# A three-block layer stack: the first two slabs multiplied without their shift, scale and norm sums in 32-column tiles, the last norm by tokens, the top-k mask on VectorE

## The reference

```python
cond = silu(c)
for i in (0, 1):                                        # first block
    sh1, sc1, g1, sh2, sc2, g2 = split(cond @ ada_w[i] + ada_b[i], 6)
    h = rms_norm(x, norm_mix[i]) * (1 + sc1) + sh1
    x = x + g1 * (stick_breaking(h, w_in, w_out) if i == 0 else dsa(h, ...))
    h = rms_norm(x, norm_ffn[i]) * (1 + sc2) + sh2
    x = x + g2 * conv_ffn(h, w_up, conv_w, conv_b, w_down)
# second block: the same frame with window attention + HGRN, and conv_ffn on the gate half
return rms_norm(x, final_norm_g)

# in dsa: 64 keys are kept for each query; of 16 heads
logits = where(selected, q @ k.T * scale + rel_bias, -1e30)
```

## Time and profile before

| | |
|---|---|
| median of the runs | 1215.47 us |
| profiled execution | 1215.8 us, of which 1214.1 us is the span from first to last instruction |
| PE | 1163.4 us busy (96%) |
| DVE | 543.6 us busy (45%) |
| ACT | 250.1 us busy (21%) |
| mean granted TensorE clock | 0.982 |
| DMA | 234.04 MB, 193 GB/s on average |

### The profile page before, as it was taken

The page is one execution under the profiler, slowest core; times in us unless marked ns, Lnnn a source line. Parts: engine busy times, 40 slices in busy tenths (PEclk is TensorE's granted clock), DMA queues, the critical chain, the costliest instruction groups (busy, mean ns, idle before and its releaser), DMA issues.

```text
span 1214.1 us, 13985 instructions
## 1 busy us (share of the span) xinstructions
PE 1163.4 (96%) x5765; PEld 1001.1 (82%) x5765; DVE 543.6 (45%) x1056; ACT 250.1 (21%) x458; POOL 23.5 (2%) x82
## 2 busy tenths in 40 slices
PE   3899999999999999998999999999999999999997
PEld 2688888888888878877888888888788888888885
DVE  6255554555564546332455546464733231111113
ACT  2122323000000244542300000025423320000002
POOL 1000140000000000000000000000000000000000
PEclk8899999999999999989999999999999999999998
DMA  9977827787868452270678787754341345353510
GB/s 347 297 260 252 300 74 275 260 312 254 308 236 302 138 70 91 83 243 1 237 254 313 251 310 262 268 184 139 110 133 36 104 131 182 110 202 105 195 47 35
DMA packets 154161, 234.04 MB, mean 193 GB/s; under 512 B 8761, under 2 KB 126577, under 8 KB 154097
## 3 DMA queue, kind: packets, MB, share of 16 engines
q1 hardware_dynamic: 154097, 233.13, 57.0%
HBM read 231.67 MB, written 1.44 MB: 192 GB/s over the span
## 4 chain that ended last, share of the span: by engine, by line
PE 94%; DVE 3%; SPq 1%; ACT 1%; issue 1%; DMA 1%; ACTq 0%; DVEq 0%
PE PS L591 49%; PE PS L658 18%; PE PS L612 7%; PE PS L602 5%; PE PS L752 2%; PE PS L577 2%; PE PS L993 1%; PE PS L563 1%; DVE ada_acc L1476 1%; DMA ffn_work<-in_final_norm_g 1%; PE PS L1067 1%; PE PS L785 1%; PE PS L922 1%; PE PS L768 1%; PE PS L804 0%
## 5 line engine op out<-in xcount | busy, mean ns | idle before, releaser
L591 PE MATMUL PS<-hT,slot 128*128 128x256 f32 x2736 | 606.2, 380 | 4.4 <-ACT hT L1176 3.1
L591 PEld LDWEIGHTS PS<-hT,slot 128*128 128x128 f32 x2736 | 520.1, 191 | 77.4 <-issue 6.8
L658 PE MATMUL PS<-act,slot 128*128 128x256 f32 x1056 | 239.2, 380 | 1.5 <-DVE act L1591 1.5
L658 PEld LDWEIGHTS PS<-act,slot 128*128 128x128 f32 x1056 | 200.1, 190 | 30.9 <-DVE act L1591 2.3
L1562 DVE TENSOR_SCALAR ffn_work<-PS,pcol 128x256 f32<-128x256 f32 x100 | 50.7, 540 | 314.3 <-PE PS L591 314.2
L1476 DVE SCALAR_TENSOR_TENSOR ada_acc<-ada_slot,cond,ada_acc 128x1024 f32<-128x1024 f32 x126 | 161.5, 1282 | 6.2 <-DMA ada_slot<-in_ada_w 0.6
L1228 ACT ACTIVATE ffn_work<-ffn_work 128x256 f32<-128x256 f32 x66 | 27.6, 418 | 615.1 <-DVE ffn_work L1572 615.1
L612 PE MATMUL PS<-oT,slot 128*128 128x256 f32 x384 | 89.5, 395 | 6.2 <-DVE oT L1788 6.2
L612 PEld LDWEIGHTS PS<-oT,slot 128*128 128x128 f32 x384 | 75.6, 199 | 18.4 <-DVE oT L1788 6.9
L602 PE MATMUL PS<-xg,slot 128*128 128x257 f32 (+1 forms) x256 | 57.4, 381 | 2.4 <-DVE xT L1526 2.4
L602 PEld LDWEIGHTS PS<-xg,slot 128*128 128x128 f32 (+1 forms) x256 | 47.6, 187 | 11.3 <-issue 4.0
(11 more groups left out here) (250 smaller groups left out, 744.3 us busy)
## 6 DMA issues: line engine op xcount, KB each, us to landing
ada_slot<-in_ada_w SPq DMA_DIRECT2D x144, 512.0 KB, 7.9
slot<-in_ffn_w_up SPq DMA_DIRECT2D x44, 1024.0 KB, 11.5
slot<-in_ffn_w_down SPq DMA_DIRECT2D x22, 1024.0 KB, 4.9
slot<-in_w_up SPq DMA_DIRECT2D x22, 1024.0 KB, 5.1
slot<-in_sb_w_in SPq DMA_DIRECT2D x12, 1024.0 KB, 7.3
slot<-in_w_in SPq DMA_DIRECT2D x11, 1024.0 KB, 5.1
slot<-in_w_down SPq DMA_DIRECT2D x11, 1024.0 KB, 4.9
slot<-in_dsa_w_in SPq DMA_DIRECT2D x10, 1024.0 KB, 5.3
```

The costliest lines, as they stand in the source:

```text
L591: last = mm(PS[:, bank, half * T:half * T + T], slot[s][:, k, m * P:(m + 1) * P], x[:, k, :], start=k == 0, stop=k == KC - 1)
L658: last = mm(PS[:, c // 2, (c % 2) * T:(c % 2) * T + T], w[:, j_odd * D + c * P:j_odd * D + (c + 1) * P], act[:, j_odd, :], start=start and ...
```

## The change

1. **Start.** Scale sums: the eight pieces of vector 1 go straight to PE, as 32-column matmuls with cond broadcast as weights (L815 of the new file), and DVE no longer passes over them. The first two slabs are multiplied by the scaled, unshifted x (`project_unshifted`), while DVE adds up vector 0 (shift). Then `shift_products` multiplies the shift by the two slabs in 32-column tiles (L616), ACT copies the rows out of PSUM, and one more matmul for each bank adds them to every token (L624). The parameter rows are issued from ACT's queue instead of SP's, slabs 0 and 1 are loaded before vector 0, and the three slabs of pass 1 have slots 3 to 5.
2. **Norm sums.** `norm` puts the eight partial sums into four positions of 32 columns; ACT copies them to SBUF, and one matmul with `quarter` (`norm_total`) adds the four. It stands behind the second matmul of the raw product that follows. GpSimd builds `quarter` before it signals `consts_ready`.
3. **dsa mask.** `sel_b` and L926 are gone; DVE adds the fp32 mask to the position bias of each pair, two additions for each pair (`masked`), and `logits` reads the masked bias.
4. **Older chunks.** In the last two pairs `was_read(1, 1)` waits for the last `mix` but one; PE starts 5 chunks of n=0, then chunk 5 of n=0 and 6 chunks of n=1, then the sixth chunk of both and 7 of n=2.
5. **Last norm.** PE transposes xT itself, chunk by chunk as it is updated; ACT sums the squares of 512 features at a time from PSUM, DVE multiplies by the inverse root and the gain (a row broadcast to all partitions, loaded during the last FFN) from PSUM, and SP stores four pieces of 256 KB.

Behind the last `mix`, 18 matmuls on older chunks now stand before the first that needs its result; before, all that followed needed it. The diff, cut to its core:

```diff
+        def sb_slot(i, s):
+
+            return s + (3 if i == 1 else 0)
...
-            load_rows(FIRST_ROWS, params_loaded)
+            load_qkv(0, (0, 1))
             load_ada(0, 0)
-            load_qkv(0)
+            load_qkv(0, (2,))
+            load_qkv(1, (0, 1))
...
+            load_ada(0, 2, range(0, 5))
+            load_qkv(1, (2,))
+            load_ada(0, 2, range(5, KC))
+            load_qkv(2, (0, 1))
+            load_ada(0, 3, range(0, 5))
+            load_qkv(2, (2,))
+            load_ada(0, 3, range(5, KC))
+            load_qkv(3, (0,))
+            load_out(0, range(2))
+            load_ada(0, 4, range(0, 5))
+            load_qkv(3, (1,))
+            load_out(0, (2,))
+            load_ada(0, 4, range(5, KC))
+            load_qkv(3, (2,))
+            load_ada(0, 5)
...
+            load_ffn_step(2, 0, 0)
+            sp.wait_ge(mixed_ready, 1)
+            g = A["final_norm_g_2"]
+            sp.dma_start(final_g[:, :], bass.AP(tensor=g.tensor, offset=g.offset, ap=[[0, P], [1, D]])).then_inc(final_loaded, 16)
+            load_ffn(2, 1)
...
+            step(pool.memset(quarter[:, :], 0.0))
+            for n in range(4):
+                step(pool.affine_select(out=quarter[:, :], in_=quarter[:, :], compare_op=ALU.not_equal, fill=1.0,
+                                        base=-32 * n, pattern=[[0, P]], channel_multiplier=1))
...
+            def shift_mods():
+
+                bk("mods_full").next()
+                pe.wait_ge(ada_used[KC - 1], bk(f"ada_used{KC - 1}").next())
+                acc = ada_acc[:, 0:D].rearrange("p (c j) -> p c j", c=KC)
+                for n in range(4):
+                    last = mm(PS[32 * n:32 * n + 32, 7, T:2 * T], ones[:, 0:32], acc[:, :, 32 * n:32 * n + 32],
+                              start=True, stop=True, skip_group_check=True)
+                last.then_inc(mods_full, 1)
...
+            def shift_products():
+
+                pe.wait_ge(shift_ready, 1)
+                for s in range(2):
+                    for k in range(KC):
+                        q = k % 4
+                        last = mm(PS[32 * q:32 * q + 32, 4 + s, 0:SLAB], mod[:, k:k + 1].to_broadcast([P, 32]), slot[s][:, k, :],
+                                  start=k < 4, stop=k >= 4, skip_group_check=True)
+                        if s == 1 and k == 0:
+                            last.then_inc(slot_used[0], 1)
+                    last.then_inc(rows_full, 1)
+                for s in range(2):
+                    pe.wait_ge(rows_ready, s + 1)
+                    for m in range(2):
+                        last = mm(PS[:, 2 * s + m, 0:T], shift_rows[:, s, m * P:(m + 1) * P],
+                                  lane[:, 0:1].to_broadcast([P, T]), start=False, stop=True)
+                        if s == 0 and m == 0:
+                            last.then_inc(slot_used[1], 1)
+                    last.then_inc(unit_full[s], 1)
...
-                    last = mm(PS[:, bank, 0:T], ones[:, :], hT[:, c, :], start=c == 0, stop=c == KC - 1)
+                    q = c % 4
+                    last = mm(PS[32 * q:32 * q + 32, bank, 0:T], ones[:, 0:32], hT[:, c, :], start=c < 4, stop=c >= 4,
+                              skip_group_check=True)
                     if c == 0 and free_slot is not None:
                         last.then_inc(slot_used[free_slot], 1)
-                last.then_inc(stat_full, 1)
+                last.then_inc(part_full, 1)
+
+            def norm_total(bank=4):
+
+                pe.wait_ge(part_ready, bk("part_ready").next())
+                mm(PS[:, bank, 0:T], quarter[:, :], part_sum[:, :], start=True, stop=True).then_inc(stat_full, 1)
...
+            def project_unshifted(bank, s, m, by_chunk=False):
+
+                for k in range(KC):
+                    if by_chunk:
+                        pe.wait_ge(scaled_ready, k + 1)
+                    mm(PS[:, bank, 0:T], slot[s][:, k, m * P:(m + 1) * P], oT[:, k, :], start=k == 0, stop=False)
...
+                    if k == 2 and total is not None:
+                        norm_total(total)
...
-            norm(FIRST)
-            mods(0, 3)
-
-            def sb_query(by_chunk=False):
-                arrived(0)
+            for k in range(KC):
+                pe.wait_ge(ada_loaded[k], 16)
+                acc = ada_slot[k].rearrange("p (c j) -> p c j", c=KC)
+                for n in range(4):
+                    last = mm(PS[32 * n:32 * n + 32, 6, T:2 * T], cond[:, k:k + 1].to_broadcast([P, 32]),
+                              acc[:, :, 32 * n:32 * n + 32], start=k == 0, stop=k == KC - 1, skip_group_check=True)
+                last.then_inc(ada_used[k], 1)
+                if k == 4:
+                    norm(FIRST)
+                elif k == 6:
+                    norm_total()
+            bk(f"ada_used{KC - 1}").next()
...
+            for s in range(2):
+                arrived(s)
+                fill(s)
+                project_unshifted(2 * s, s, 0, by_chunk=s == 0)
+                project_unshifted(2 * s + 1, s, 1)
+            shift_mods()
+            shift_products()
+            sb_value(0)
...
-                    mm(PS[:, 4 + e, 0:P], qh[:, b, e, 0:P], kn[:, 0:P], start=False, stop=False, skip_group_check=True)
-                    mm(PS[:, 4 + e, P:384], qh[:, b, e, P:T], kn[:, :], start=False, stop=False, skip_group_check=True)
-                if p == 0:
-                    pe.wait_ge(sel_ready, 1)
-                for e in range(2):
-                    last = mm(PS[:, 4 + e, 0:384], ident_b[:, :], sel_b[:, :], start=False, stop=True, skip_group_check=True)
+                    mm(PS[:, 4 + e, 0:P], qh[:, b, e, 0:P], kn[:, 0:P], start=False, stop=True, skip_group_check=True)
+                    last = mm(PS[:, 4 + e, P:384], qh[:, b, e, P:T], kn[:, :], start=False, stop=True, skip_group_check=True)
...
-                    was_read(1)
-                    out_start(1, 0, 6)
+                    was_read(1, 1)
+                    out_start(1, 0, 5)
                 else:
-                    was_read(1)
-                    out_start(1, 1, 7)
+                    was_read(1, 1)
+                    out_products(1, 0, (5,))
+                    out_start(1, 1, 6)
                 turn(p, frees=1 if p == 5 else None)
                 if p < 7:
                     scores(p + 1)
                 mix(p)
 
+            was_read(1, 1)
+            out_products(1, 0, (6,))
+            out_products(1, 1, (6,))
+            out_start(1, 2, 7)
             was_read(1)
-            out_projection(1, started=(6, 7))
+            out_projection(1, started=(7, 7, 7))
...
+            for c in range(KC):
+                pe.wait_ge(x_turned, c + 1)
+                for tt in range(2):
+                    last = pe.transpose(PS[:, 4 + 2 * tt + c // 4, (c % 4) * P:(c % 4) * P + P],
+                                        xT[:, c, tt * P:(tt + 1) * P], ident[:, :])
+                    if c % 4 == 3:
+                        last.then_inc(unit_full[2 + tt], 1)
...
+                act_e.wait_ge(part_full, bk("part_full").next())
+                act_e.activation(part_sum[:, :], PS[:, bank, 0:T], ACT.Copy).then_inc(part_ready, 1)
...
+            for t, row, n, rows_of in FIRST_ROWS:
+                act_e.dma_start(prow[row:row + n, t, :], rows_of).then_inc(params_loaded, 16)
...
+            bk("scaled_ready").next(KC)
+            act_e.wait_ge(shift_ready, 1)
+            for s in range(2):
+                act_e.wait_ge(rows_full, s + 1)
+                act_e.activation(shift_rows[:, s, :], PS[:, 4 + s, 0:SLAB], ACT.Copy).then_inc(rows_ready, 1)
+            for c in range(KC):
+                act_e.activation(hT[:, c, :], oT[:, c, :], ACT.Identity, bias=mod[:, c:c + 1]).then_inc(h_ready, 1)
...
+            act_e.preload_act_table(ACT.Sqrt)
+            for half in range(2):
+                for tt in range(2):
+                    full(2 + tt)
+                    act_e.activation(sq_flat[:, (2 * half + tt) * 512:(2 * half + tt + 1) * 512], PS[:, 4 + 2 * tt + half, :],
+                                     ACT.Square, scale=D ** -0.5,
+                                     accum_out=ss[:, tt, half:half + 1]).then_inc(ss_ready, 1)
+                    if half:
+                        act_e.wait_ge(ss_ready, 3 + tt)
+                        act_e.wait_ge(ss_eps_ready, tt + 1)
+                        act_e.activation(rtok[:, tt:tt + 1], ss[:, tt, 1:2], ACT.Sqrt, bias=ss[:, tt, 0:1]).then_inc(rtok_ready, 1)
...
+            dve.wait_ge(ada_used[KC - 1], 1)
+            ins = vector_sum(6, 1)
+            link(ins)
+            link(dve.scalar_tensor_tensor(gain[:, 0:KC], mod[:, KC:2 * KC], 1.0, col("norm_mix0", 0, KC), ALU.add, ALU.mult))
+            dve.wait_ge(rstd_ready, bk("rstd_ready").next())
+            for c in range(KC):
+                dve.scalar_tensor_tensor(oT[:, c, :], xT[:, c, :], gain[:, c:c + 1], rstd[:, :], ALU.mult, ALU.mult)\
```

(42 more changed lines are left out.)

153 lines of the change are left out of this document (81 added, 72 removed).

## The result

The changed kernel takes 1182.76 us in the median of four runs (1180.95 to 1184.52), the kernel before 1215.43 us: a ratio of 0.974, 95% interval 0.9721 to 0.9759. Forecast: 1179.5 us, between 1173.5 and 1189. Timed again on another chip (label after_again), it took 1179.53 us (1179.37 to 1182.0), a ratio of 0.9721 (0.9707 to 0.9736). The four runs of the first session lie in two pairs, 1181 and 1184.5 us; the trace is of the first pair. The profiled execution took 1180.95 us, its span is 1179.1 us.

The account below looks back on a forecast made before the run. PE's own work, busy 1163.4 us of a 1214.1 us span, plus 50.7 us idle was taken as the bound. Six terms sum to 36.2 us off the profiled 1215.8: 1179.6, stated as 1179.5 us, range 1173.5 to 1189.

Parts of the forecast that it names:

- start: Start: PE sums the scale, shift deferred; slab 2 starts at 44.6 instead of 53.63 us, 9.0 us gained.
- last norm: Kernel's end: new last norm ends at 1207.3 us, 6.8 us gained, bounds 5.3 and 8.
- three FFN norms: FFN norms: tiled sums save PE 2.0 us each and all of it stays, 6.0 us gained.
- two mixer norms: Mixer norms: the root is critical, so 1.2 us stay of each saving, 2.5 us gained.
- mask: dsa pairs: dropping L926 saves 0.42 us in each of six pairs, DVE's additions hidden; 2.5 us gained.
- older chunks: End of dsa, last mixes to FFN: 9.4 us gained if a 1.8 us wait leaves the clock up.
- The chain behind vector 0: Start, between DVE's sum of vector 0 and slab 2: a chain with nothing beside it, 6.4 us.
- The wait of 0.8 us in the mixers: Mixer norms: PE would be at hT's first chunk at 429.2, ready at 429.95, and waits 0.8 us.
- The rival in which the clock falls: Clock falls after dsa's 1.8 us wait and during the start, losing 3.0 and 2.4 us: 1185; chance 0.17.
- No slab was late in passes 1 to 3: Against the loads rival: loads set when slabs of passes 1 to 3 land, start's gain lost: 1188.5; chance 0.09.
- The tiles ran side by side: Against the tiles rival: in norms and start each 32-column tile costs a full matmul: 1200; chance 0.05.

Follow-up runs that it names:

- u_chunks: Changed kernel with the last two sparse-attention pairs as before, PE waiting for the newest copy ahead of 6 and 7 chunks: 1192.31 us.
- shift_first: Changed kernel with the shift added by ScalarE before the first two slabs' products, no row products, scale sums still on PE: 1193.35 us.
- sums_dve: Changed kernel with the scale vector's sums back on DVE ahead of the shift vector, the shift still added as rows: 1180.11 us.
- moved_pair: Changed kernel with the query slab multiplied ahead of the first window scores instead of behind them: 1178.6 us.
- pair_and_sums: Changed kernel with the query slab ahead of the first window scores and the scale sums on DVE: 1177.99 us.
- u_norm: Changed kernel with the five later mid norms summed in eight full products again, without ACT copy and total; first norm unchanged: 1188.93 us.
- u_mask: Changed kernel with the sparse-attention mask back on PE and DVE's two additions per pair gone: 1181.04 us, repeated on another chip 1180.42 us.
- u_tail: Changed kernel with the last norm as before, in columns with full-width sums, transposes, two copies and two stores: 1188.66 us.
- pair_and_rows: Changed kernel with the query slab ahead of the first window scores and the parameter rows transposed behind three pieces' sums: 1178.22 us.
- one_position: Changed kernel with each norm's eight 32-column tiles all on the first column position, in one chain: 1197.26 us.

## Why the prediction was right, step by step

The mechanisms were right, and the six terms nearly so in the one execution that was traced (1180.95 us). The median, 1182.76, is 3.3 us above the forecast, in good part because two of the four runs took 1184.5, and none of these was traced. The sum is also closer than its terms: start and last norm gave 2.2 us more than forecast, the other four 1.7 less, and a loss of 1.6 came where nothing was forecast. Gained between the two profiled executions, at the positions behind each part:

| term | forecast | measured | undone alone |
|---|---|---|---|
| start | 9.0 | 10.4 | only in halves |
| three FFN norms | 6.0 | 5.4 | 5.5 |
| two mixer norms | 2.5 | 2.3 | 2.2 |
| mask | 2.5 | 1.8 | 1.9 |
| older chunks | 9.4 | 9.2 | 10.4, 1.2 of it the mask's additions |
| last norm | 6.8 | 7.6 | 7.6 |
| cross products near 906 us, not forecast | 0 | -1.6 | |
| sum | 36.2 | 35.1 | |

*Start.* Slab 0 was put at 22.1 us and stood at 20.57, waiting for its own load, which landed 0.15 us behind the first scaled chunk; the scale sums ended at 18.2, not 20.2, because PE kept pace with the pieces. That was this execution's luck: with the same start, slab 0 began at 20.5 to 22.8 us and slab 2 up to 2.0 us later in the traces of the other kernels, so the term is 8.4 to 10.4. The chain behind vector 0 took 43.25 - 36.71 = 6.5 us, forecast 6.4. One step was mis-sized: vector 0 was to be added up at 35.5, 2.7 us ahead of the slabs' end, and was ready at 36.66, 0.3 behind it. So at best it, and not slab 0, sets how early slab 2 can be. In the trace of u_chunks the two slabs took 14.08 us and were done at 34.6, and PE then idled 2.45 us for DVE.

What the step did not see: its two halves are worth very different things. Without the deferred shift this start is *later* than the one before (shift_first: 18.69 us of idle PE), where vector 0 is loaded behind two slabs. With it, the sums on TensorE move slab 0 by up to 1.8 us. At slab 2 that is 2.5 us against the trace of the changed kernel (sums_dve) and 0.1 us against that of moved_pair (pair_and_sums), and in time nothing shows. The new load order was not undone in any run.

*Norms.* 2.0 us was 0.2 too much. The total moves what follows by 0.43 us, as forecast; its row of 0.59 counts an end that overlaps. The tiles cost 1.20 instead of 1.00: from one record to the next PE takes 0.22 us, but 0.31 into the first tile and 0.32 behind the product after the last. The four records of a group start within 0.03 us of each other. The wait of 0.8 us in the mixers was forecast and is 0.84. ACT's table load took 1.28 us, 0.02 us behind the copy, and Ln still waited 0.60 us for PE's total. By the rule of the Trainium skill (ScalarE: Activation LUTs, What ACT_TABLE_LOAD costs), 2.66 us with the drain, Ln would have come 0.8 us later than it did, by estimate; the trace disagrees again. Eight tiles on four positions took 1.07 us and on one 3.64, 3.4 times as long; the Trainium skill (TensorE: Matmul & The Clock Gate, Why this matters for your kernels) has 2.38 times for three.

*Mask.* 0.32 us a pair instead of 0.42: L926's two products are gone, but the mix now starts 0.53 us behind the last product of the scores, where L926 started 0.44 behind it. DVE's additions were hidden, as forecast; its slack is down to 0.42 us. They do delay the copy of the mix by 1.17 us (u_chunks), which the forecast did not name and which costs nothing here.

*Older chunks.* The wait was put at 1.8 us and is 1.39, with the clock at 1.00 behind it; one of 0.29 was not forecast. The rival in which the clock falls did not come here. The forecast took from two rows that a wait this short leaves the clock up. Length alone does not decide it: behind the 1.95 us before the cross products the clock fell in three of 14 traces (last section).

*Last norm.* The end follows DVE's last update by 7.7 us, not 8.5: DVE's last product ends 5.3 us behind it (1175.28 + 1.41), where 5.8 were set, and the last store takes 2.4 instead of 2.7 us.

*Rivals.* No slab was late in passes 1 to 3: PE's only wait for a slab is the one at 20.57. The tiles ran side by side. The clock's rival was right in kind: the clock fell near 906 us, where the change had edited nothing, and in the trace of u_chunks in the shift products of the start (L616 3.11 instead of 1.93 us).

## What to carry to other kernels

A product that is linear in a late input can start without it and take the late part as a small product behind it; what its companion edits are worth is then asked again, with the main one in place. Small sums gain by lying on four column positions, where a copy and a short total find cover elsewhere. Work that an idle engine takes over can stand ahead of something else that is waited for; that it is free holds only with the other edits in place. A term of 2 us in 1180 is read by positions in a trace: medians of four runs moved here by more, at places that no edit had touched.

## What the runs showed of the hardware

**One wait, two prices.** The window scores stand behind a wait of 2.71 to 2.74 us in 11 traces. In four of these (u_norm, both of u_mask, sums_dve) scores and next slab took 9.55 us, in the other seven (that of the kernel before among them) 11.0 to 11.2, with the granted clock down to 0.50. The two kernels that were traced twice, the changed one and u_mask, each showed the same price both times. First the changed kernel, then u_norm:

```profile
839.38 0.93 PE L1114 MATMUL PS<-kT,qT 64*128 64x128 f32 x8 [2.71 <-DVE vtok L2067]
...
842.55 8.02 PE L668 MATMUL PS<-hT,slot 128*128 128x256 f32 x32
```
```profile
846.97 0.93 PE L1117 MATMUL PS<-kT,qT 64*128 64x128 f32 x8 [2.71 <-DVE vtok L2071]
...
849.45 7.07 PE L671 MATMUL PS<-hT,slot 128*128 128x256 f32 x32
```

So it is with the cross products of the recurrence (L1207 to L1209, near 906 us), behind a wait of 1.95 us: 2.95 us in 11 traces, 4.57 in 3 (the changed kernel, u_tail, pair_and_rows). Each costs 1.6 us or nothing. These places do not account for the 3.5 us between the runs of the changed kernel at 1181 and those at 1184.5: the traced execution, of 1180.95 us, paid both prices already, and its start was at its best, so only the start's 2 us are left. The mean granted clock of the two slower runs is 0.991, that of the others 0.994 and 0.996, which points to the clock; but none of them was traced, so where they lost it stays open, as does what decides the clock behind equal waits.

**Half pace at a full clock.** Behind the turned parameter rows, the first 20 scale tiles (40 records) took 2.37 us in some traces and 3.82 to 4.17 in others (u_norm, moved_pair, u_tail; 4.43 in one_position), though the granted clock is 1.00 in both. The rows' own transposes took 0.42 to 0.43 us where the tiles took 2.37 (0.60 in u_chunks), and 0.65 elsewhere. PE had idled 0.35 to 1.15 us for the rows where the tiles took 2.37, and 0.58 to 1.31 elsewhere, so the idle time alone does not tell them apart. The cause stays open.
